# Gated-linear-attention and MoBA trunk on one core: the order of the first loads and of the first two projection blocks

## The chip, the cores and the metric

The kernel runs on one core of a Trainium2 chip. The metric is device time in microseconds (us) for one launch, the median of the runs of one program. The core has five instruction streams: TensorE (PE, matrix products into PSUM), VectorE (DVE), ScalarE (ACT), GpSimd (POOL) and SyncE (SP). They run apart and meet in semaphores. In this kernel SP and POOL do little else than issue DMA transfers, each on a queue of its own.

## What is computed

Two residual layers over x of 256 x 1024 in float32; layer 0 mixes with gated linear attention, layer 1 with MoBA attention, and each mixer is followed by a squared-ReLU MLP. Every sublayer is RMS-normed and modulated by vectors that come from c. The part that matters here is the beginning:

```python
c_act = jax.nn.silu(c)
mod = (c_act @ ada_w[i] + ada_b[i])[:, None, :]
sh1, sc1, g1, sh2, sc2, g2 = jnp.split(mod, 6, axis=-1)
h = rms_norm(x, norm_mix_g[i]) * (1 + sc1) + sh1
...
q, k, v, r, glr = jnp.split(h @ w_in, splits, axis=-1)
g = jax.nn.log_sigmoid((glr @ w_gate_up + b_gate).astype(f32)) / GLA_GATE_NORM
...
G = jnp.cumsum(g.reshape(B, NC, L, H, DK), axis=2)
q_dec = q * jnp.exp(G)
k_inv = k * jnp.exp(-G)
```

## The kernel before

**Tiling.** The 256 tokens are two tiles of 128 partitions, the contraction of 1024 is eight chunks of 128. A projection of 1024 by 512 columns is a *block* n; it is cut into four *units* u of two chunks each. Each weight number is split into a rounded part (`w_hi`, made on ACT, line 860) and the rest (`w_lo`, made on DVE, line 1186), the activations likewise (`a_hi`, `a_lo`), and three products are summed, so a unit costs 12 matmuls of 128 x 512 (lines 428 to 430, helper `three`). Units are counted through the whole kernel. `w_raw` holds four pieces of two units, `w_hi` and `w_lo` four units.

**Layer 0, mixer.** Blocks 0 to 5 are k, q, v, v, r, r (`MIX_IN`), 6 and 7 the output. Their results lie in PSUM banks 4 to 7, two for each block. Among the units, `sides` puts other TensorE work: for block 0, `second_mods` after unit 1 and `glr` after unit 3; for block 1, `logits` after unit 0 and `turn_k` after unit 2; then `turn_q`, `turn_tail`, `scores`, `update` and `output`. The gate's chain goes `glr` (TensorE), its copy (ACT, inside `k_in`), `logits` (TensorE), the bias and `z` (DVE `logits`), exp and ln (ACT `softplus`), the running sum (DVE `cumulate`), the exponentials (ACT `decays`), `keys` and `queries` (DVE), `scores` (TensorE). ACT and DVE have tables `tasks` that place these steps after a given (block, unit) of their splitting, and DVE a table `slots` with the places of the sums of the later modulation vectors (`ada`, lines 1201 and 1204), four instructions of 128 x 512 each.

**The modulation vectors of the first norm.** Four blocks of 512 columns of `ada_w` (0, 2, 1, 3 in this order, `ADA_PE`) are multiplied on TensorE: `ada_rows` gives rows spread over partitions 0, 32, 64 and 96 of one bank, ACT copies them (`ada_out`, line 900), and `ada_cols` sums them into columns. Blocks 0 and 2 belong to the first half of the channels (activation chunks 0 to 3, units 0 and 1 of every block), blocks 1 and 3 to the second half. `modulate` on ACT and DVE then makes `a_hi` and `a_lo`. Pieces of `w_raw` are called by block and half: piece (0, 0) holds units 0 and 1 of block 0.

**Queues.** SP issues, in this order: c, the identity, `ada_w` block 0, x, seven small vectors (`rows`), `ada_w` block 2, piece (0, 0), `ada_w` block 1, `ada_w` block 3, piece (0, 1), `constants` (the two gate weights `glr_w` and `glr_up`, masks, the restart vector of 512 KB, gate biases of 1 MB), then pieces (1, 0), (1, 1) and so on. POOL loads `ada_w` blocks from 4 on into `ada_raw`, as its halves come free.

## Time and profile before

| what | value |
| --- | --- |
| time, median of 3 runs | 687.27 us (686.78 to 690.5) |
| span of the profiled execution, first to last instruction | 686.4 us |
| lowest time minus that span | 0.4 us |
| TensorE busy | 646.6 us, 94% of the span |
| DVE busy | 470.6 us, 69% |
| ACT busy | 338.4 us, 49% |
| POOL busy | 30.3 us, 4% |
| DMA | 156.87 MB, mean 229 GB/s |
| mean granted TensorE clock | 0.980 |

No time of its own was taken of the profiled execution; its span stands for it, 0.4 us below the lowest time and 0.9 us below the median. Busy shares are averages over stages. The change touches the first tenth or so of the span; what it is worth there is read from the timelines of the three engines, from what each waited for, and from how long each transfer took to land. Times below are in us from the start of the span.

### The profile page before, as it was taken

How to read it: one execution, taken by the hardware profiler on the slowest of the kernel's cores; microseconds unless marked ns; L12 is line 12 of the kernel's file. 1: busy time of each engine (PE TensorE's matmuls, PEld its weight loads, DVE VectorE, ACT ScalarE, POOL GpSimd, SP SyncE). 2: the span in 40 equal slices, each digit the busy share in tenths (PEclk: the TensorE clock that was granted, in tenths of full speed). 3: DMA queues.
4: the chain of work that ended last, by engine and by line, in shares of the span. 5: the costliest groups of instructions: out<-in, count | busy, mean ns of one | idle time of the engine just before them, and what ended most of it. 6: DMA issues, size and time to landing. Idle time of an engine off the chain costs nothing.

```text
span 686.4 us, 9712 instructions
## 1 busy us (share of the span) xinstructions
PE 646.6 (94%) x3594; PEld 535.0 (78%) x3594; DVE 470.6 (69%) x702; ACT 338.4 (49%) x562; POOL 30.3 (4%) x44
## 2 busy tenths in 40 slices
PE   4789999999999999999997999989999999999997
PEld 2457866677789988998885666667779998999885
DVE  2358999696787877787886846685678844555446
ACT  3244632544854345435427756665585445443440
POOL 0011010000000000000000000000000000000000
PEclk9889999999999999999999999999999999999999
DMA  8999778554598877878935677760349555565501
GB/s 305 380 377 352 244 265 309 198 176 154 181 317 311 296 250 270 317 258 287 343 118 183 221 270 246 259 230 1 123 145 336 193 185 187 184 182 198 195 32 61
DMA packets 61492, 156.87 MB, mean 229 GB/s; under 512 B 4124, under 2 KB 5000, under 8 KB 61464
## 3 DMA queue, kind: packets, MB, share of 16 engines
q1 hardware_dynamic: 50584, 114.56, 48.3%
q0 software_dynamic: 10880, 41.95, 17.5%
q8 instruction: 17, 0.28, 0.2%
q14 instruction: 11, 0.09, 0.0%
HBM read 155.44 MB, written 1.05 MB: 228 GB/s over the span
## 4 chain that ended last, share of the span: by engine, by line
PE 77%; DVE 12%; ACT 6%; DMA 2%; issue 2%; SPq 1%; ACTq 0%; DVEq 0%; POOLq 0%
PE ps L428 16%; PE ps L429 15%; PE ps L430 15%; PE ps L582 8%; PE ps L581 8%; PE ps L580 8%; DVE w_lo L1186 3%; ACT w_hi L860 2%; PE ps L488 2%; DVE ada_acc L1204 1%; DMA rows<-in_ada_b_dram 1%; DMA ada_raw<-in_ada_w_dram 1%; DVE a_lo L1329 1%; PE ps L512 1%; PE ps L496 1%
## 5 line engine op out<-in xcount | busy, mean ns | idle before, releaser
L1186 DVE TENSOR_TENSOR w_lo<-w_raw,w_hi 128x1024 fp32r<-128x1024 f32 x192 | 232.4, 1222 | 140.7 <-ACT w_hi L860 140.5
L860 ACT ACTIVATE w_hi<-w_raw 128x1024 fp32r<-128x1024 f32 x192 | 200.4, 1057 | 222.7 <-PE ps L430 116.8
L428 PE MATMUL ps<-w_hi,a_hi 128*128 128x512 f32 x288 | 121.1, 421 | 20.1 <-DVE a_lo L1329 14.1
L580 PE MATMUL ps<-a_hi,w_hi 128*128 128x256 f32 x448 | 126.9, 283 | 0.0
L582 PE MATMUL ps<-a_hi,w_lo 128*128 128x256 f32 x448 | 126.8, 283 | 0.0
L581 PE MATMUL ps<-a_lo,w_hi 128*128 128x256 f32 x448 | 126.8, 283 | 0.0
L429 PE MATMUL ps<-w_lo,a_hi 128*128 128x512 f32 x288 | 116.0, 403 | 0.0
L430 PE MATMUL ps<-w_hi,a_lo 128*128 128x512 f32 x288 | 115.5, 401 | 0.0
L428 PE MATMUL ps<-w_hi,m_hi 128*128 128x512 f32 x256 | 100.7, 393 | 0.0
L429 PE MATMUL ps<-w_lo,m_hi 128*128 128x512 f32 x256 | 100.4, 392 | 0.0
L430 PE MATMUL ps<-w_hi,m_lo 128*128 128x512 f32 x256 | 100.3, 392 | 0.0
L428 PEld LDWEIGHTS ps<-w_hi,a_hi 128*128 128x128 f32 x288 | 56.2, 195 | 47.2 <-issue 16.9
L1204 DVE SCALAR_TENSOR_TENSOR ada_acc<-ada_raw,c_act,ada_acc 128x512 f32<-128x512 f32 (+1 forms) x112 | 84.0, 750 | 3.5
L581 PEld LDWEIGHTS ps<-a_lo,w_hi 128*128 128x128 f32 x448 | 85.9, 192 | 0.6
L580 PEld LDWEIGHTS ps<-a_hi,w_hi 128*128 128x128 f32 x448 | 85.9, 192 | 0.5
L582 PEld LDWEIGHTS ps<-a_hi,w_lo 128*128 128x128 f32 x448 | 85.9, 192 | 0.0
L430 PEld LDWEIGHTS ps<-w_hi,a_lo 128*128 128x128 f32 x288 | 56.2, 195 | 12.5
L429 PEld LDWEIGHTS ps<-w_lo,a_hi 128*128 128x128 f32 x288 | 56.3, 196 | 10.6 <-issue 0.2
L428 PEld LDWEIGHTS ps<-w_hi,m_hi 128*128 128x128 f32 x256 | 48.5, 190 | 11.2 <-issue 1.4
L430 PEld LDWEIGHTS ps<-w_hi,m_lo 128*128 128x128 f32 x256 | 48.5, 189 | 10.2
L429 PEld LDWEIGHTS ps<-w_lo,m_hi 128*128 128x128 f32 x256 | 48.5, 189 | 9.6
L284 POOL DMA_DIRECT2D ada_raw<-in_ada_w_dram x38 | 28.5, 749 | 452.5 <-DVE ada_acc L1204 359.0
(158 smaller groups left out, 509.1 us busy)
## 6 DMA issues: line engine op xcount, KB each, us to landing
w_raw<-in_mlp_w_dram SPq DMA_DIRECT2D x64, 1024.0 KB, 5.4
ada_raw<-in_ada_w_dram POOLq DMA_DIRECT2D x40, 1024.0 KB, 6.0
w_raw<-in_gla_w_in_dram SPq DMA_DIRECT2D x12, 1024.0 KB, 11.1
w_raw<-in_moba_w_in_dram SPq DMA_DIRECT2D x12, 1024.0 KB, 6.3
ada_raw<-in_ada_w_dram SPq DMA_DIRECT2D x4, 1024.0 KB, 10.8
arena<-in_ada_w_dram SPq DMA_DIRECT2D x4, 1024.0 KB, 12.8
w_raw<-in_gla_w_out_dram SPq DMA_DIRECT2D x4, 1024.0 KB, 7.7
w_raw<-in_moba_w_out_dram SPq DMA_DIRECT2D x4, 1024.0 KB, 5.1
```

The costliest lines, as they stand in the source:

```text
L284: nc.gpsimd.dma_start(ada_raw[:, half], src.rearrange("(k p) n -> p k n", p=P)).then_inc(ada_sw_in[half], 16)
L428: mm(out, hi, w_hi[:, slot, wc], start=first, stop=False)
L429: mm(out, hi, w_lo[:, slot, wc], start=False, stop=False)
L430: return mm(out, lo, w_hi[:, slot, wc], start=False, stop=last)
L488: z = mm(ps[32 * k:32 * k + 1, bank, :], c_act[:, 4 * half + k:4 * half + k + 1], raw[:, k], start=half == 0, stop=half == 1)
L496: z = mm(ps[:, bank, c0 + q:c0 + q + 1], ada_row[i // 4][:, i % 2, q * P:(q + 1) * P], ones[0:97, 0:1], start=True, stop=True)
L580: mm(o, w_hi[:, u, w], a_hi[:, a, :], start=u == 0 and k == 0, stop=False)
L581: mm(o, w_hi[:, u, w], a_lo[:, a, :], start=False, stop=False)
L582: z = mm(o, w_lo[:, u, w], a_hi[:, a, :], start=False, stop=u == 3 and k == 1)
L860: A(w_hi[:, c % SPLIT], w_raw[:, c // 2, c % 2], ACT.Copy).then_inc(hi_made, 1)
L1186: V.tensor_tensor(w_lo[:, c % SPLIT], w_raw[:, c // 2, c % 2], w_hi[:, c % SPLIT].bitcast(F32), ALU.subtract).then_inc(lo_made, 1)
L1204: z = V.scalar_tensor_tensor(acc, w, s, acc, op0=ALU.mult, op1=ALU.add)
```

## The change

- SP: x goes ahead of `ada_w` block 0. The order is now c, identity, x, `ada_w` 0, `ada_w` 2, piece (0, 0), `ada_w` 1, piece (1, 0), `ada_w` 3, piece (0, 1), piece (1, 1), and on from there.
- POOL: the seven small vectors are its first issues; the gate weights, then (behind `ada_w` block 4) the other constants and the gate biases follow.
- TensorE: x is transposed before the first `ada_rows`; the first two blocks run as (0,0), (0,1), (1,0), (1,1), (0,2), (0,3), (1,2), (1,3), with the `ada_rows` of block 1 after (0,1), those of block 3 and both `ada_cols` after (1,1), `glr` after (0,3), `logits` after (1,2).
- ACT: in `first_norm` it now does both x tiles first; the last two `ada_out` follow the splitting of units 2 and 3. The third and fourth row sums are in banks 0 and 1, and a column `sel` with ones in four partitions takes the place of `ones` in `ada_cols`.
- Tasks and slots of ACT and DVE in blocks 1 to 3 are moved to later units.

The order of ACT in the program, before. The stretch from the first `modulate` to the splits of units 4 and 5 (L860 is the split of a unit, L900 `ada_out`, L890 and L894 `modulate`):

```order
L894 ACTIVATE a_hi<-arena 128x512 [waits hD_ok,hA_ok]
L900 ACTIVATE arena<-ps 97x512 [waits col_T,ada_pe]
L860 ACTIVATE w_hi<-w_raw 128x1024 [waits raw_in1]
L860 ACTIVATE w_hi<-w_raw 128x1024
L900 ACTIVATE arena<-ps 97x512 [waits col_T,ada_pe]
L890 ACTIVATE arena<-ps,modc 128x256 [waits xT_ok,mod_ok]
L894 ACTIVATE a_hi<-arena 128x512 [waits hD_ok,hA_ok]
L890 ACTIVATE arena<-ps,modc 128x256 [waits xT_ok,mod_ok]
L894 ACTIVATE a_hi<-arena 128x512 [waits hD_ok,hA_ok]
L860 ACTIVATE w_hi<-w_raw 128x1024 [waits unit_used,raw_in2]
L860 ACTIVATE w_hi<-w_raw 128x1024 [waits unit_used]
```

The same stretch after the change (L883 is the split, L922 `ada_out`, L912 and L916 `modulate`):

```order
L916 ACTIVATE a_hi<-arena 128x512 [waits hD_ok,hA_ok]
L883 ACTIVATE w_hi<-w_raw 128x1024 [waits raw_in1]
L883 ACTIVATE w_hi<-w_raw 128x1024
L922 ACTIVATE arena<-ps 97x512 [waits col_T,ada_pe] x2
L912 ACTIVATE arena<-ps,modc 128x256 [waits xT_ok,mod_ok]
L916 ACTIVATE a_hi<-arena 128x512 [waits hD_ok,hA_ok]
L912 ACTIVATE arena<-ps,modc 128x256 [waits xT_ok,mod_ok]
L916 ACTIVATE a_hi<-arena 128x512 [waits hD_ok,hA_ok]
L883 ACTIVATE w_hi<-w_raw 128x1024 [waits unit_used,raw_in2]
L883 ACTIVATE w_hi<-w_raw 128x1024 [waits unit_used]
```

The row order hardly moved, but the units did: before, the two splits in front of the second `modulate` are units (0,2) and (0,3); now they are (1,0) and (1,1), and those of (0,2) and (0,3) stand behind it.

DVE before, from its `logits` (L1361, L1364) over `cumulate` (L1370 to L1375) and `keys` (L1383, L1384) to `queries` (L1390, L1393); L1186 is the split, L1201 and L1204 are `ada`:

```order
L1361 TENSOR_SCALAR arena<-ps,cols 128x256 x4
L1364 SCALAR_TENSOR_TENSOR arena<-arena 128x1024
L1201 TENSOR_SCALAR ada_acc<-ada_raw,c_act 128x512
L1204 SCALAR_TENSOR_TENSOR ada_acc<-ada_raw,c_act,ada_acc 128x512 x3
L1186 TENSOR_TENSOR w_lo<-w_raw,w_hi 128x1024
L1370 SCALAR_TENSOR_TENSOR arena<-arena 128x1024
L1372 SCALAR_TENSOR_TENSOR arena<-arena 128x1024
L1375 TENSOR_TENSOR arena<-arena 128x1024
L1186 TENSOR_TENSOR w_lo<-w_raw,w_hi 128x1024 x2
L1383 TENSOR_TENSOR arena<-ps,arena 128x512
```

DVE after, the same steps (L1382 and L1385 `logits`, L1391 to L1396 `cumulate`, L1404 `keys`, L1208 the split, L1223 and L1226 `ada`):

```order
L1382 TENSOR_SCALAR arena<-ps,cols 128x256 x4
L1385 SCALAR_TENSOR_TENSOR arena<-arena 128x1024
L1208 TENSOR_TENSOR w_lo<-w_raw,w_hi 128x1024
L1391 SCALAR_TENSOR_TENSOR arena<-arena 128x1024
L1393 SCALAR_TENSOR_TENSOR arena<-arena 128x1024
L1396 TENSOR_TENSOR arena<-arena 128x1024
L1208 TENSOR_TENSOR w_lo<-w_raw,w_hi 128x1024
L1404 TENSOR_TENSOR arena<-ps,arena 128x512
L1405 TENSOR_TENSOR arena<-ps,arena 128x512
L1404 TENSOR_TENSOR arena<-ps,arena 128x512
L1405 TENSOR_TENSOR arena<-ps,arena 128x512
L1208 TENSOR_TENSOR w_lo<-w_raw,w_hi 128x1024
```

The `ada` group left the place between `logits` and `cumulate`; it now stands behind `keys`, between the splits of units (3,0) and (3,1), and one split fewer stands between `cumulate` and `keys`.

TensorE after, from the program's start to the first product (L519 the transposes of x, L495 `ada_rows`, L503 `ada_cols`); before, the eight `ada_rows` of block 0 and the turn of `rows` came first and the sixteen transposes behind the first `ada_cols`:

```order
L519 MATMUL ps<-eye,arena 128x128 [waits xn_ok]
L519 MATMUL ps<-eye,arena 128x128 x7
L519 MATMUL ps<-eye,arena 128x128 [waits xn_ok]
L519 MATMUL ps<-eye,arena 128x128 x7
L495 MATMUL ps<-ada_raw,c_act 1x512 [waits ada_in0,set_up,c_ok]
...
L531 MATMUL ps<-eye,rows 128x100 [waits vec_in]
L495 MATMUL ps<-arena,c_act 1x512 [waits ada_pre_in0]
...
L503 MATMUL ps<-sel,arena 128x1 [waits row_ok]
...
L495 MATMUL ps<-arena,c_act 1x512 [waits ada_pre_in1]
...
L503 MATMUL ps<-sel,arena 128x1 [waits row_ok,vec_ok]
```

The transposes moved ahead of everything that waits for `ada_w`.

The diff, cut to what the text speaks of:

```diff
+    FIRST = [(0, 0), (0, 1), (1, 0), (1, 1), (0, 2), (0, 3), (1, 2), (1, 3)]
+    FIRST_DONE = [6, 8]
...
+            def vec(at, n, src):
+                nc.gpsimd.dma_start(rows[at:at + n, :], src).then_inc(vec_in, 16)
...
+            pool.wait_ge(ada_pe, 4)
+            with nc.allow_non_contiguous_dma(reason="sixteen columns"):
+                nc.gpsimd.dma_start(glr_w[:, :, :],
...
+            nc.gpsimd.dma_start(glr_up[:, :], gla_up[0]).then_inc(glr_in, 16)
             for half in range(2):
                 pool.wait_ge(ada_pe, 6 + half + 1)
                 nc.gpsimd.dma_start(ada_raw[:, half], ada_part(4, half)).then_inc(ada_sw_in[half], 16)
+            nc.gpsimd.dma_start(restart.rearrange("p a b -> p (a b)"), restart_d.to_broadcast([P, GH * SEQ])
+                                ).then_inc(con_in, 16)
...
+            for tb in range(TB):
+                sp.dma_start(x[:, tb], x_d[0, tb * P:(tb + 1) * P, :]).then_inc(x_in[tb], 16)
             for half in range(2):
                 load_ada(0, half)
-            for tb in range(TB):
-                sp.dma_start(x[:, tb], x_d[0, tb * P:(tb + 1) * P, :]).then_inc(x_in, 16)
...
+            load_pre(0, 2)
...
+                order = [(n, d) for n in range(MIX_BLOCKS) for d in range(2)]
+                if l == 0:
+                    order[1:3] = [(1, 0), (0, 1)]
...
+                    if l == 0 and i == 0:
+                        load_pre(1, 1)
+                    if l == 0 and i == 1:
+                        for half in range(2):
+                            load_ada(3, half)
...
             def first_norm():
+                for tb in range(TB):
+                    turn_norm(0, tb)
                 pe.wait_ge(c_ok, 1)
-                pe.wait_ge(set_up, 2)
+                pe.wait_ge(set_up, 3)
                 for half in range(2):
                     ada_rows(0, half, 6)
                 pe.wait_ge(vec_in, 16 * N_VEC)
                 tr(ps[:, 5, 0:N_ROWS], rows[0:N_ROWS, :], eye[0:N_ROWS, 0:N_ROWS]).then_inc(vec_T, 1)
+                ada_rows(2, 0, 7)
                 ada_cols(0, 4)
-                for tb in range(TB):
-                    turn_norm(0, tb)
-                for half in range(2):
-                    ada_rows(2, half, 7)
+                ada_rows(2, 1, 7)
...
+                def first_blocks(sides):
+
+                    for s, (n, u) in enumerate(FIRST):
+                        pe.wait_ge(lo_made, mix_base[0] + s + 1)
+                        if n == 0:
+                            pe.wait_ge(a_ok, u + 1)
...
+                first_blocks({1: lambda: second_rows(2), 3: lambda: (second_rows(3), second_cols()),
+                              5: glr, 6: logits})
...
-                    (1, 3): [k_in],
-                    (2, 0): [softplus],
+                    (2, 1): [k_in],
+                    (2, 2): [softplus],
...
-                    (2, 0): [logits], (2, 1): [cumulate], (2, 3): [keys], (3, 1): [queries, zero],
+                    (2, 1): [logits], (2, 2): [cumulate], (2, 3): [keys], (3, 1): [queries, zero],
...
-                slots = [(1, 0), (1, 2), (2, 0), (3, 1), (3, 2), (3, 3), (4, 0), (4, 2), (5, 0), (5, 2)]
+                slots = [(1, 3), (2, 0), (3, 0), (3, 1), (3, 2), (3, 3), (4, 0), (4, 2), (5, 0), (5, 2)]
```

## Rows read from the trace of the kernel before

**Rows 1.** The page's first part: busy us, share of the span, instructions of each engine.

```profile
PE 646.6 (94%) x3594; PEld 535.0 (78%) x3594; DVE 470.6 (69%) x702; ACT 338.4 (49%) x562; POOL 30.3 (4%) x44
```

**Rows 2.** Timeline of TensorE before the first product: start, duration, instruction, idle.

```profile
13.88 0.43 PE L522 MATMUL ps<-eye,rows 100*128 100x100 f32 x1 [2.21 <-DMA rows<-in_ada_b_dram]
...
15.71 3.65 PE L512 MATMUL ps<-eye,arena 128*128 128x128 f32 x16
19.30 2.90 PE L488 MATMUL ps<-arena,c_act 128*1 128x512 f32 x16
```

**Rows 3.** SP's issue of piece (0, 0), 8 to 9, and its time to landing.

```profile
L322 SPq DMA_DIRECT2D w_raw<-in_gla_w_in_dram x1: 1110/1110/1110, 8.1 to 8.1; - x1
...
DMA to landing us min/median/max: 13.1/13.1/13.1
```

**Rows 4.** Timeline of ACT, around both norms' halves and softplus.

```profile
22.76 1.99 ACT L860 ACTIVATE w_hi<-w_raw 128x1024 fp32r<-128x1024 f32 x2
...
43.44 0.63 ACT L894 ACTIVATE a_hi<-arena 128x512 fp32r<-128x512 f32 x1
...
63.56 1.06 ACT L962 ACTIVATE arena<-arena 128x1024 f32<-128x1024 f32 x1 [4.12 <-DVE arena L1364]
64.66 1.06 ACT L963 ACTIVATE arena<-arena 128x1024 f32<-128x1024 f32 x1
```

**Rows 5.** Timeline of TensorE, 27 to 66: where each stage of blocks 0 and 1 begins.

```profile
27.84 0.77 PE L428 MATMUL ps<-w_hi,a_hi 128*128 128x512 f32 x1 [3.80 <-DVE w_lo L1186]
...
35.21 1.90 PE L488 MATMUL ps<-arena,c_act 128*1 128x512 f32 x16
...
38.76 1.05 PE L496 MATMUL ps<-ones,arena 97*128 97x1 f32 x8
40.20 1.05 PE L496 MATMUL ps<-ones,arena 97*128 97x1 f32 x8 [0.39 <-ACT arena L900]
43.82 0.77 PE L428 MATMUL ps<-w_hi,a_hi 128*128 128x512 f32 x1 [2.57 <-DVE a_lo L1329]
...
51.72 3.63 PE L647 MATMUL ps<-arena,glr_w 128*16 128x256 f32 x16
...
60.14 0.50 PE L428 MATMUL ps<-w_hi,a_hi 128*128 128x512 f32 x1
...
65.73 1.04 PE L660 MATMUL ps<-eye,arena 128*128 128x128 f32 x8
```

**Rows 6.** Windows by time: PE, PEld, DVE, ACT, POOL busy, then granted clock, DMA.

```profile
46.00:48.00 2.00, 2.00 (x6) 1.54 (x6) 1.49 (x2) 1.43 (x2) 0.00 (x0) 0.50 1.03 385
104.00:105.00 1.00, 1.00 (x4) 0.71 (x4) 0.96 (x3) 0.00 (x0) 0.00 (x0) 0.50 1.01 401
```

**Rows 7.** Timeline of DVE, 60 to 80: `logits`, `ada`, `cumulate`, `keys`, `queries`.

```profile
60.62 1.65 DVE L1361 TENSOR_SCALAR arena<-ps,cols 128x256 f32<-128x256 f32 x4
62.30 1.23 DVE L1364 SCALAR_TENSOR_TENSOR arena<-arena 128x1024 f32<-128x1024 f32 x1
63.45 0.48 DVE L1201 TENSOR_SCALAR ada_acc<-ada_raw,c_act 128x512 f32<-128x512 f32 x1
63.96 2.33 DVE L1204 SCALAR_TENSOR_TENSOR ada_acc<-ada_raw,c_act,ada_acc 128x512 f32<-128x512 f32 x3
...
67.84 1.22 DVE L1370 SCALAR_TENSOR_TENSOR arena<-arena 128x1024 f32<-128x1024 f32 x1
...
72.56 2.35 DVE L1186 TENSOR_TENSOR w_lo<-w_raw,w_hi 128x1024 fp32r<-128x1024 f32 x2
74.83 0.68 DVE L1383 TENSOR_TENSOR arena<-ps,arena 128x512 f32<-128x512 f32 x1
...
79.58 1.28 DVE L1393 SCALAR_TENSOR_TENSOR arena<-ps,arena 128x512 f32<-128x512 f32 x2
```

**Rows 8.** Timeline of TensorE, 79 to 145: the first wait for DVE's state.

```profile
101.92 1.10 PE L700 MATMUL ps<-arena 64*128 64x256 f32 x6 [1.71 <-DVE arena L1416]
```

**Rows 9.** POOL's two loads of `ada_w` block 4, issued at 38.3 and 39.2.

```profile
DMA to landing us min/median/max: 9.0/10.6/12.2
```

More of the change, by code:

```diff
@@ L100, in trunk_kernel @@
         cols = sb("cols", [P, P])
+        sel = sb("sel", [P, 1])
         c_act = sb("c_act", [P, KC])
@@ L496, in ada_cols @@
                     z = mm(ps[:, bank, c0 + q:c0 + q + 1], ada_row[i // 4][:, i % 2, q * P:(q + 1) * P],
-                           ones[0:97, 0:1], start=True, stop=True)
+                           sel[0:97, :], start=True, stop=True)
                 z.then_inc(col_T, 1)
@@ L718, in output, with second_rows, second_cols @@
                     z.then_inc(o_p, 1)
-                def second_mods():
+                def second_rows(i):
+                    for half in range(2):
+                        ada_rows(ADA_FIRST[i], half, i - 2)
+                def second_cols():
                     for i in range(2, 4):
-                        for half in range(2):
-                            ada_rows(ADA_FIRST[i], half, 4 + i)
-                    for i in range(2, 4):
-                        ada_cols(i, 4 + i)
-                sides = [{1: second_mods, 3: glr},
-                         {0: logits, 2: turn_k},
-                         {1: turn_q, 2: turn_tail, 3: scores},
-                         {2: lambda: update(0), 3: lambda: update(1)},
+                        ada_cols(i, i - 2)
+                def first_blocks(sides):
[3 more added lines that the diff above has]
+                            pe.wait_ge(a_ok, u + 1)
+                        if (n, u) == (0, 2):
+                            pe.wait_ge(mod_red, 4)
+                        for k in range(2):
+                            for tb in range(TB):
+                                z = three(ps[:, in_bank(n, tb), :], a_hi[:, 2 * u + k, tile(tb)],
+                                          a_lo[:, 2 * u + k, tile(tb)], s % SPLIT, slice(k * COLS, (k + 1) * COLS),
+                                          u == 0 and k == 0, u == 3 and k == 1)
+                        z.then_inc(unit_used, 1)
+                        if s in sides:
+                            sides[s]()
+                sides = [None, None,
+                         {0: turn_k, 1: turn_q, 3: turn_tail},
+                         {0: scores, 2: lambda: update(0), 3: lambda: update(1)},
                          {0: lambda: update(2), 1: lambda: update(3), 2: lambda: output(0), 3: lambda: output(1)},
@@ L917, in first_norm @@
             def first_norm():
-                ada_out(0)
                 for tb in range(TB):
                     squares(0, tb)
-                ada_out(1)
+                for i in range(2):
+                    ada_out(i)
                 for u in range(2):
@@ L1657, in _ @@
             V.memset(ones[:, :], 1.0).then_inc(set_up, 1)
+            link(V.memset(sel[:, :], 0.0))
+            for k in range(4):
+                z = V.memset(sel[32 * k:32 * k + 1, :], 1.0)
+            z.then_inc(set_up, 1)
             V.memset(ps[:, 6:8, :], 0.0).then_inc(set_up, 1)
```

88 lines of the change are left out of this document (35 added, 53 removed).

## The prediction

> **What bounds the kernel now.** I read the page's busy shares first: TensorE works for 94% of the span, so 40 us are idle, and DVE is next with 69% [rows 1]. Such shares say nothing of a stage, so I went to TensorE's timeline of the first 66 us. Two gaps stand out there: 3.80 us before the first product at 27.84, and 2.57 us (with 0.39 just ahead) before the product of unit (0,2) at 43.82 [rows 5]. The third view is the timeline of DVE from 60 on: its rows join almost without a hole from `logits` to `queries` [rows 7], and TensorE's next long wait is one for DVE, 1.71 us before the `update` at 101.92 [rows 8]. So three things set the end of this stage in turn: transfers and the modulation up to 43.82, TensorE itself up to about 60, and then, although TensorE seems busy, the gate's chain on DVE up to 101.92. DVE has no slack there, and that decides this change. From 101.92 on nothing in the program is ordered otherwise, so whatever DVE is late or early there moves the end by as much.
>
> **The change, part 1: the start.** TensorE does the sixteen transposes of x (3.65 us) and waits 2.21 us for the small vectors ahead of the row sums of `ada_w` 2, which start at 19.30 and take 2.90 [rows 2]. Both leave the path. What is late next? Each half of those sums needs its own megabyte, landed by 19.30 at the latest, since no idle time stands there. In the new order only the second half (half of 2.90, 1.45 us) and ACT's copy of 0.6 stand behind that landing: 21.3. Piece (0, 0) was issued at 8.1 and took 13.1, so it is there at 21.2 [rows 3], and the bytes ahead of it are the same in both orders. ACT's first split begins at 22.76 now [rows 4] and at about 21.3 then. The gain is 22.76 - 21.3 = 1.5 us, and all that follows to the first product comes along: 27.84 becomes 26.3. I take 1.5. Its bounds are 0 (the vectors or x come no sooner than they are wanted) and 2.2 (the whole wait for the vectors, if the pieces land sooner as well).
>
> The small vectors go to POOL's queue. The nearest row is POOL's two loads of `ada_w` 4, issued while SP's queue was full: 9.0 and 12.2 us to landing [rows 9], for a megabyte each. If the last vectors, issued at about 6, took those 12.2, they would land at 18.2, TensorE would then turn them and do both halves of the sums (0.43 + 2.90, and the column sums of 1.05 between), and nearly all of the 1.5 us would be gone: 695.6 instead of the 694.3 below. I take no delay, because they are 8 KB and not 1024 KB each. By the Trainium skill (DMA: Bandwidth & Descriptors, section Queues, rings and completion order) each DMA engine takes turns between the queues it has work for, packet by packet, so small vectors on a queue of their own do not stand behind SP's megabytes; by that rule the gain stays whole. No row of before shows small transfers on POOL's queue.
>
> The memsets for `sel` are five more instructions on DVE in a stretch where it has nothing else to do. `sel` for `ones` changes no size. Both cost nothing; without that cover they would be well under 1 us.
>
> **Part 2: the first two blocks, interleaved.** From the first product to `glr` the program now takes 51.72 - 27.84 = 23.9 us [rows 5]. The new order, stage by stage, with the same rows: units (0,0), (0,1) 35.21 - 27.84 = 7.4; sums of `ada_w` 1, half of 38.76 - 35.21, 1.8; units (1,0), (1,1), 24 products at full clock, 65.73 - 60.14 = 5.6; sums of `ada_w` 3, 1.8; column sums, second `modulate`, up to the next product, 43.82 - 38.76 = 5.1; units (0,2), (0,3) 51.72 - 43.82 = 7.9. That is 29.6, so 5.7 us more ahead of `glr`. The 5.6 of them that are the moved units are no loss for TensorE, which does the work sooner, but they are a delay for all that waits for `glr`.
>
> Something is added. Before, units (0,2) and (0,3) are split ahead of the second `modulate`; now their splits are units 4 and 5 of ACT's and DVE's order and stand behind it. ACT's last `modulate` step ends at 44.07 [rows 4]; then the split on ACT takes 1.0 (half of 1.99) and its rest on DVE 1.2 (half of 2.35) [rows 4, 7]: 46.3 instead of 43.82, 2.5 us more. So TensorE's second gap does not close; it grows from 2.57 to about 5. The clock was at 0.50 after the present gap (46 to 48) [rows 6], which is the 1.2 GHz level, and the 7.9 above hold that cost already; it is paid again.
>
> `glr` therefore moves by 5.7 + 2.5 - 1.5 = 6.7 us. From it to the end of the `logits` products the pieces are the same as before (`glr`, one unit, `logits`, 8.4 us up to 60.14) [rows 5]. DVE picked the result up at 60.62, not 60.2, since it was busy with a split; then it will be waiting. So DVE's `logits` starts at 66.9, 6.3 later.
>
> **Part 3: the moved tasks.** Before, the `ada` group (63.45 to 66.29, 2.8 us) and a split lie between `logits` and `cumulate`, which starts at 67.84 although ACT's exp and ln were done at 65.72 [rows 4, 7]. In the new table only one split of 1.2 us lies there, so `cumulate` starts when ACT is done: 2.1 us less. Between `cumulate` and `keys` one split is left instead of two (2.35 us), but `keys` must wait for two of ACT's exponentials, of some 1.05 each like those of softplus [rows 4], so nothing is gained. Then the `ada` group comes ahead of `queries`: 2.8 us more. In sum +0.7. `queries`, over at 79.58 + 1.28 = 80.86 before [rows 7], is over at 80.86 + 6.3 + 0.7 = 87.9. TensorE now places `scores` after unit (3,0): by the stages above it is there at about 86, so it waits some 2 us for DVE. From `queries` on DVE's table is the old one, so the 7.0 us stay: `update` at 101.92 becomes 108.9, and the end moves by 7.0.
>
> The sum: -1.5 + 5.7 + 2.5 - 0.4 + 0.7 = +7.0 us on the profiled span of 686.4, which was 0.4 below the lowest time and 0.9 below the median. On the median: 687.27 + 7.0 = 694.3.
>
> **Part 4: POOL's other transfers.** The masks, the restart vector and the gate biases, 1.9 MB, leave the space ahead of pieces (1, 0) and (1, 1), and stand behind `ada_w` 4 on POOL. First user is `cumulate`, at about 72; they are issued near 44. At 395 GB/s [rows 6] they take 4.8 us, so they are hidden. The first `ada` of DVE wants `ada_w` 4 at about 52: issued at about 42, it lands between 51 and 54 [rows 9]. DVE then has about 4 us free before `logits` at 66.9, which covers that.
>
> **The rivals.** (1) Only TensorE's own work counts, and DVE catches up. One split less stands behind `logits`, and DVE idles before it, which speaks for it; the closed rows of DVE and the wait at 101.92 speak against it. Then the end moves by -1.5 + 0.1 + 2.5 = +1.1: 688.4. (2) Faster. TensorE arrives at the `update` with 5.6 us of work done in advance, so if DVE's chain were not late, the wait of 1.71 [rows 8] and the slow clock behind it (0.50 at 104 [rows 6], nine products at 0.43 instead of 0.23 us, 1.8) would vanish: 688.4 - 3.5 = 684.9, and 684.2 with the larger start gain. It decides from the point at which `glr` moves by less than DVE's gain of 2.1; I find 6.7, so this needs the two units before `glr` to be nearly free. (3) It does not do what it says: the first product comes at 27.8 as before, because vectors or x hold it. Then 687.27 + 8.5 = 695.8. (4) POOL's queue becomes the bound: `ada_w` 4 lands late, because the gate weights (64-byte runs) and SP's pieces share the engines with it, DVE stands in its order, and the splits queued behind that `ada` keep TensorE waiting. With one more landing time of the shorter kind left over after the 4 us of cover, 9.0 - 4 - 2 = 3 us: 697.3.
>
> **Chances.** Forecast 0.66, with 692.3 to 696.3 as its own range; rival (1) 0.12; (2) 0.07; (3) 0.07; (4) 0.08. About 0.5%, 3.4 us, is what a measurement of this kernel can tell from no change. Slower by more than that is above 690.7: forecast, (3) and (4), 0.81. Within it are (1) and most of (2), 0.15. Faster by more is 0.04. The range goes from 690.0, which takes in the upper part of (1), to 698.0, which takes in (3) and (4).
>
> **What would show it.** In the new profile: the first product near 26.3; a second gap of about 5 us before unit (0,2) at about 50.5, put down to a split (`w_lo`) and no longer to `a_lo`; `glr` near 58.4; DVE's `logits` near 66.9 with some 4 us idle ahead; TensorE waiting about 2 us for `queries` at `scores`; the first `update` that waits for the state near 108.9; and equal stages from there. The forecast is wrong if the interleaved units run while the clock stays at full speed without a second gap, if `logits` comes before 64, or if DVE reaches `queries` with slack.

## The result

The changed kernel takes 694.06 us, the median of 4 runs (692.91 to 695.7); the kernel before took 687.67 in the 4 runs beside it (686.78 to 690.5). The ratio is 1.0081, 95% interval 1.0051 to 1.011: slower by 0.8%. Between the medians that is 6.4 us, by the ratio 5.6 us (3.5 to 7.6). The forecast was 694.3. In the profiled executions the span grew by less, from 686.4 to 691.7, 5.3 us; where the rest went is one of the questions below. The profiled execution of after took 693.48 us, so 1.8 us of it lie outside the span.

The first row of its page, to be held against [rows 1]. TensorE is busy for less time than before in a span that is longer, so the loss is idle time and not work:

```profile
PE 644.0 (93%) x3594; PEld 532.8 (77%) x3594; DVE 471.1 (68%) x707; ACT 338.6 (49%) x562; POOL 38.4 (6%) x59
```

The timeline of TensorE after: start, duration, instruction, and in brackets the idle time before it with what ended it. Line numbers are those of after (L435 is the first product of a unit, L654 `glr`, L691 `scores`, L707 `update`, L718 `output`):

```profile
14.34 0.31 PE L531 MATMUL ps<-eye,rows 100*128 100x100 f32 x1
...
26.46 0.77 PE L435 MATMUL ps<-w_hi,a_hi 128*128 128x512 f32 x1 [4.90 <-DVE w_lo L1208]
...
43.09 1.95 PE L503 MATMUL ps<-sel,arena 97*128 97x1 f32 x16
50.11 0.79 PE L435 MATMUL ps<-w_hi,a_hi 128*128 128x512 f32 x1 [5.07 <-DVE w_lo L1208]
...
57.51 3.63 PE L654 MATMUL ps<-arena,glr_w 128*16 128x256 f32 x16
...
86.99 2.05 PE L691 MATMUL ps<-arena 128*128 128x128 f32 x16 [1.71 <-DVE arena L1414]
...
98.65 2.07 PE L707 MATMUL ps<-arena 64*128 64x256 f32 x6 [3.41 <-DVE arena L1426]
...
118.05 0.70 PE L718 MATMUL ps<-arena 128*128 128x256 f32 x2 [0.36 <-DVE arena L1437]
```

Against [rows 5] and [rows 8]: the first product comes 1.4 us earlier; the second gap has doubled and is put down to a split, `w_lo`; `glr` is 5.8 us later; TensorE waits for `queries` at `scores`. One row is not in the prediction at all: the wait of 3.41 us at the first `update`, for `masked` (L1426).

DVE's timeline after (L1382 `logits`, L1391 `cumulate`, L1223 the first of an `ada` group, L1414 `queries`, L1426 `masked`, L1437 the state), to be held against [rows 7]:

```profile
66.04 1.66 DVE L1382 TENSOR_SCALAR arena<-ps,cols 128x256 f32<-128x256 f32 x4 [4.51 <-PE ps L660]
71.17 1.23 DVE L1391 SCALAR_TENSOR_TENSOR arena<-arena 128x1024 f32<-128x1024 f32 x1 [1.08 <-ACT arena L985]
...
81.67 0.48 DVE L1223 TENSOR_SCALAR ada_acc<-ada_raw,c_act 128x512 f32<-128x512 f32 x1
...
85.65 1.28 DVE L1414 SCALAR_TENSOR_TENSOR arena<-ps,arena 128x512 f32<-128x512 f32 x2
...
93.37 0.49 DVE L1223 TENSOR_SCALAR ada_acc<-ada_raw,c_act 128x512 f32<-128x512 f32 x1 [1.20 <-DMA ada_raw<-in_ada_w_dram]
97.27 1.32 DVE L1426 COPY_PREDICATED arena<-keep,ps 128x512 f32<-128x512 int32 x2
...
103.47 0.49 DVE L1223 TENSOR_SCALAR ada_acc<-ada_raw,c_act 128x512 f32<-128x512 f32 x1 [0.75 <-DMA ada_raw<-in_ada_w_dram]
108.35 0.48 DVE L1437 SCALAR_TENSOR_TENSOR arena<-arena,dec,ps 128x256 f32<-128x256 f32 x1
```

DVE is idle for 4.5 us ahead of `logits`, since TensorE brings its input late. From there to the state its holes are short, the longest of them 1.20 us. The state is ready at 108.8; before, at 101.8.

Two windows of 2 us each at the end of the next norm, in after and then in before (PE, PEld, DVE, ACT, POOL busy, then granted clock, DMA share, GB/s):

```profile
160.00:162.00 2.00, 2.00 (x16) 1.85 (x16) 1.97 (x5) 0.00 (x0) 0.00 (x0) 1.00 0.97 369
162.00:164.00 2.00, 2.00 (x11) 1.62 (x10) 1.93 (x4) 0.00 (x0) 0.00 (x0) 1.00 0.94 342
```

```profile
154.00:156.00 2.00, 2.00 (x9) 1.71 (x9) 1.93 (x5) 0.00 (x0) 0.00 (x0) 0.62 1.00 395
156.00:158.00 2.00, 2.00 (x6) 1.51 (x6) 1.79 (x3) 0.00 (x0) 0.00 (x0) 0.53 1.03 388
```

It is the same work in both. Before, the clock was at its lower level for most of 4 us, which costs (1 - 0.62) x 2 + (1 - 0.53) x 2 = 1.7 us; in this execution of after it stayed at full speed. From 134.7 up to that place TensorE's rows are 6.7 us late, behind it 5.1 us. So the forecast of +7.0 was nearly met up to here, and 1.6 us came back through the clock in this one execution.

### The profile page after: what moved, and what is told of

It reads as the page before. It is cut to its first block, busy times and chain, and to the rows that moved or that the text cites. A ratio compares the mean times of both kernels' runs of the same rounds, so it can differ in the third digit from the quotient of the medians.

```text
span 691.7 us, 9715 instructions
## 1 busy us (share of the span) xinstructions
PE 644.0 (93%) x3594; PEld 532.8 (77%) x3594; DVE 471.1 (68%) x707; ACT 338.6 (49%) x562; POOL 38.4 (6%) x59
## 4 chain that ended last, share of the span: by engine, by line
PE 75%; DVE 12%; ACT 5%; DMA 4%; issue 2%; SPq 1%; ACTq 0%; POOLq 0%; DVEq 0%
PE ps L435 16%; PE ps L436 15%; PE ps L437 15%; PE ps L589 8%; PE ps L588 8%; PE ps L587 8%; DVE w_lo L1208 3%; DMA w_raw<-in_gla_w_in_dram 2%; DMA ada_raw<-in_ada_w_dram 2%; PE ps L495 2%; ACT w_hi L883 1%; DVE ada_acc L1226 1%; DVE a_lo L1350 1%; PE ps L718 1%; DVE x L1362 1%
## 5 line engine op out<-in xcount | busy, mean ns | idle before, releaser
L1208 DVE TENSOR_TENSOR w_lo<-w_raw,w_hi 128x1024 fp32r<-128x1024 f32 x192 | 232.4, 1223 | 130.5 <-ACT w_hi L883 130.3
L883 ACT ACTIVATE w_hi<-w_raw 128x1024 fp32r<-128x1024 f32 x192 | 200.3, 1057 | 227.8 <-PE ps L437 122.1
L435 PE MATMUL ps<-w_hi,a_hi 128*128 128x512 f32 x288 | 121.0, 420 | 24.1 <-DVE w_lo L1208 12.6
L435 PE MATMUL ps<-w_hi,m_hi 128*128 128x512 f32 x256 | 100.7, 393 | 0.0
L435 PEld LDWEIGHTS ps<-w_hi,a_hi 128*128 128x128 f32 x288 | 55.8, 194 | 52.5 <-issue 17.2
L1226 DVE SCALAR_TENSOR_TENSOR ada_acc<-ada_raw,c_act,ada_acc 128x512 f32<-128x512 f32 (+1 forms) x112 | 84.0, 750 | 3.5
L435 PEld LDWEIGHTS ps<-w_hi,m_hi 128*128 128x128 f32 x256 | 48.5, 190 | 11.2 <-issue 1.4
```

The lines of the kernel that those rows point to most:

```text
L435: mm(out, hi, w_hi[:, slot, wc], start=first, stop=False)
L883: A(w_hi[:, c % SPLIT], w_raw[:, c // 2, c % 2], ACT.Copy).then_inc(hi_made, 1)
L1208: V.tensor_tensor(w_lo[:, c % SPLIT], w_raw[:, c // 2, c % 2], w_hi[:, c % SPLIT].bitcast(F32), ALU.subtract).then_inc(lo_made, 1)
L1226: z = V.scalar_tensor_tensor(acc, w, s, acc, op0=ALU.mult, op1=ALU.add)
```

## The experiments

Each experiment was timed in 5 rounds beside the kernel before on the same chip; ratios are to that one, and 0.1% is 0.7 us. The row of after is the measurement above. The theory is that of the prediction: DVE's chain from `logits` to the state, which now begins late, sets the end. Its main rival is that only TensorE's own gap counts.

| kernel | ratio to before (95% interval) | span |
| --- | --- | --- |
| after | 1.0081 (1.0051 to 1.0110) | 691.7 |
| e1_start_only | 1.0017 (0.9997 to 1.0036) | 686.6 |
| e2_interleave_only | 1.0106 (1.0086 to 1.0126) | 693.0 |
| e3_split_ahead | 1.0049 (1.0032 to 1.0067) | 689.6 |
| e4_ada_in_gap | 1.0063 (1.0042 to 1.0083) | 692.8 |
| e6_before_ada_late | 0.9943 (0.9924 to 0.9963) | 683.3 |
| e7_start_ada_late | 0.9976 (0.9962 to 0.9990) | 685.6 |
| e8_after_ada_late | 0.9989 (0.9973 to 1.0005) | 689.8 |
| e10_glr_first | 0.9922 (0.9901 to 0.9942) | 682.1 |
| e11_start_table_late | 0.9933 (0.9911 to 0.9955) | 684.5 |
| e12_start_const_late | 0.9933 (0.9907 to 0.9959) | 683.8 |
| e13_split_ada_late | 0.9956 (0.9934 to 0.9979) | 683.2 |
| e14_const_on_pool | 0.9971 (0.9952 to 0.9991) | 687.4 |

**The two halves of the change.** e1 is the kernel before with the new start alone (x first, small vectors on POOL, x turned first; the constants stay on SP's queue):

```diff
+            for tb in range(TB):
+                sp.dma_start(x[:, tb], x_d[0, tb * P:(tb + 1) * P, :]).then_inc(x_in[tb], 16)
             for half in range(2):
                 load_ada(0, half)
...
+                for tb in range(TB):
+                    turn_norm(0, tb)
                 pe.wait_ge(c_ok, 1)
```

> The kernel before with the start of the change alone (x first, small vectors on POOL, transposes first), blocks 0 and 1 not interleaved, constants still on SP. Theory (DVE's chain, fed by the pieces of block 1, ends the stage): the first product comes at 26.4 instead of 27.84, but pieces (1, 0) and (1, 1) land at 45 and 52 as before, DVE closes up behind them, the update that waits for the state is at 101.5 to 101.9, and the end moves by 0 to -0.5 us. Rival (the start gain is passed on whole, as it was in the changed kernel): the update is at 100.4 and the end moves by -1.4 us.

Its first product comes at 26.59, 1.25 us earlier than before, and its state is waited for until 102.02, later than before [rows 8]:

```profile
102.02 1.10 PE L700 MATMUL ps<-arena 64*128 64x256 f32 x6 [1.86 <-DVE arena L1414]
```

The gain is made and does not arrive. At `glr` it is already gone (51.67 against 51.72), and in this trace all of it went on TensorE, without a wait: units (0,0) and (0,1) took 8.2 us instead of 7.4, units (0,2) and (0,3) 8.3 instead of 7.9. The clock stayed at its lower level for longer. The window from 30 to 32, in e1 and then in before:

```profile
30.00:32.00 2.00, 2.00 (x6) 1.52 (x6) 0.00 (x0) 0.00 (x0) 0.00 (x0) 0.50 1.05 386
```

```profile
30.00:32.00 2.00, 2.00 (x7) 1.53 (x7) 0.00 (x0) 0.00 (x0) 0.00 (x0) 0.60 1.05 386
```

The time of e1 is 1.2 us above before, with an interval from -0.2 to +2.5. That leaves out the rival's -1.4 and takes in the upper end of the theory's range (0), but the trace does not show the theory's reason: DVE's `logits` starts 8.9 us behind `glr` as in before, so DVE was not late by itself. The trace is of one of the three shortest of the twelve executions of e1 (688.3 us; the median is 690.78), so what makes the others longer it does not show.

e2 is the changed kernel with the old start:

> The changed kernel with the old start (ada_w 0 ahead of x, small vectors on SP, transposes behind the first sums); interleaving, tasks, slots and constants as changed. Theory: first product at 27.8, glr 1.4 us later than in the changed kernel (58.9), and the end 1.4 us above the changed kernel, +7.8 us over the kernel before. Rival (the start has no part in it): the end is that of the changed kernel, +6.4.

It is 0.25% above after, with intervals that overlap, so the times alone don't tell the theory from its rival. In the trace each mark from the first product on (27.61) is 1.2 us later than in after: `glr` 58.66, DVE's `logits` 67.18, and the span is 1.3 us longer. The row of its second gap:

```profile
51.28 0.80 PE L436 MATMUL ps<-w_hi,a_hi 128*128 128x512 f32 x1 [5.08 <-DVE w_lo L1209]
```

So the loss is the interleaving's (1.06% alone, 7.3 us), and in the traces the start gains its 1.2 us there, where it does not gain in e1.

**The size of the second gap.** e3 puts the splits of units (0,2) and (0,3) back ahead of the second `modulate`:

```diff
-                for i in range(2, 4):
-                    ada_out(i)
+                ada_out(2)
+                for u in range(4, 6):
+                    hi_at(u)
+                ada_out(3)
...
-                for u in range(2, 4):
+                for u in range(2, 6):
```

> The changed kernel with the splits of units (0,2) and (0,3) moved ahead of the second modulate on ACT and DVE. Theory: the gap before unit (0,2) shrinks from 5.1 to 2.6 us, glr starts at 55.0 instead of 57.5, DVE's logits, queries and the update all come 2.5 us sooner, and the end 2.5 us below the changed kernel (691.6). Rival (TensorE's own work is the bound and the chain on DVE is not): the gap shrinks, but waits further on grow by the same amount and the end stays within 0.7 us.

```profile
47.56 0.47 PE L435 MATMUL ps<-w_hi,a_hi 128*128 128x512 f32 x1 [2.53 <-DVE a_lo L1353]
```

The gap is 2.53 again and put down to `a_lo` again, and the kernel gains 0.32%, 2.2 us. The unit comes 2.55 us earlier than in after, and all of that is the gap: the first product is 0.9 us earlier (25.53), but TensorE is slower behind it, and the column sums begin at 43.09 in both. The difference has some 2.4 us either way; e13 against e8 below makes the same edit and gives 2.3 us with 1.9 either way. The two together confirm the term of 2.5 us as a cause.

**The chain on DVE.** e4 moves the `ada` group that now stands ahead of `queries` into DVE's idle time before `logits`:

```diff
-                    (2, 1): [logits], ...
+                    (2, 1): [lambda: ada(5, 0), logits], ...
```

> The changed kernel with one ada group (ada_w 5, first half) moved from behind keys to ahead of DVE's logits, where DVE sits idle for 4.5 us. Theory (DVE's chain decides): logits is at most 0.8 us later, queries about 2.0 us sooner (85.0 instead of 86.9), and the end about 2 us below the changed kernel (692.1). Rival (TensorE is the bound, scores has slack): queries comes sooner, the end stays within 0.5 us. Rival (the load of ada_w 5 is late, since it stands behind the constants on POOL's queue): logits waits for it, 2 us or more later, and the end rises.

```profile
65.57 0.49 DVE L1223 TENSOR_SCALAR ada_acc<-ada_raw,c_act 128x512 f32<-128x512 f32 x1 [4.64 <-DMA ada_raw<-in_ada_w_dram]
```

The idle time is there, but the data is not: this `ada_w` block lands at 65.5, so `logits` starts at 68.34 instead of 66.04 and most of the 2.8 us is given back. The verdict on the time is open, since its interval overlaps that of after. What it shows is that the hole on DVE is no free place, as the queue that fills it is as late as the hole.

e6, e8 and e13 take the opposite way: the groups go behind the chain. Only the table changes, in e6 of the kernel before, in e8 of after, and in e13 of e3:

```diff
-                slots = [(1, 0), (1, 2), (2, 0), (3, 1), (3, 2), (3, 3), (4, 0), (4, 2), (5, 0), (5, 2)]
+                slots = [(1, 0), (1, 2), (2, 0), (3, 1), (3, 3), (4, 0), (4, 2), (5, 0), (5, 1), (5, 2)]
...
-                slots = [(1, 3), (2, 0), (3, 0), (3, 1), (3, 2), (3, 3), (4, 0), (4, 2), (5, 0), (5, 2)]
+                slots = [(1, 3), (2, 0), (3, 1), (3, 3), (4, 0), (4, 2), (5, 0), (5, 1), (5, 2), (5, 3)]
```

> The kernel before with one ada group taken off DVE's closed stretch: the places (3, 2) and (3, 3) become (3, 3) and (4, 0), and so on, the last new one being (5, 1), so that four groups and not five lie between logits and the state; nothing else. Theory (DVE's chain ends the stage at 101.92): the state comes about 3 us sooner, the 1.7 us wait at the update and the slow clock behind it go, and the end moves by -2.5 to -4 us. Rival (TensorE is the bound of the stage, DVE's wait is incidental): the wait goes but the end moves by less than 1 us.

> The changed kernel with the ada groups moved off DVE's stretch (places (1, 3), (2, 0), (3, 1), (3, 3), (4, 0), (4, 2), (5, 0), (5, 1), (5, 2), (5, 3)); interleaving and start as changed. Theory (of the 6.4 us most is the chain on DVE, and 2.5 is the late split on TensorE): queries comes 2.9 us sooner, the waits at scores and at the first update go or shrink, and the end falls by 5 to 6.5 us, to 0 to +1.5 over the kernel before. Rival (TensorE's own longer way is the main part): the end falls by less than 3 us.

> The changed kernel with both the splits of units (0,2) and (0,3) ahead of the second modulate (as in e3_split_ahead) and the later ada table of e8_after_ada_late. Theory: the 2.2 us of the splits and the 6.4 us of the table add up, since each is on the path and neither hides the other: ratio to before 0.995 to 0.996. Rival: with DVE given slack by the table TensorE is the bound, and the split's 2.5 us come only in part or, by TensorE's own gap, still in full; if they come in no part the ratio stays at 0.9989.

In e6 the third `update` starts with no wait:

```profile
100.21 1.13 PE L700 MATMUL ps<-arena 64*128 64x256 f32 x6
```

It saves 0.57%, 3.9 us, where the chain's wait and the slow products behind it came to 1.7 + 1.7 us in the trace of before. In e8 `glr` and `logits` are even 1.4 us later than in after (58.87 and 67.39), and yet DVE ends `masked` at 92.9 instead of 98.6, and the wait of 3.41 us is gone:

```profile
84.24 1.28 DVE L1414 SCALAR_TENSOR_TENSOR arena<-ps,arena 128x512 f32<-128x512 f32 x2
...
91.55 1.35 DVE L1426 COPY_PREDICATED arena<-keep,ps 128x512 f32<-128x512 int32 x2
```

```profile
93.83 1.13 PE L707 MATMUL ps<-arena 64*128 64x256 f32 x6
...
102.52 1.10 PE L707 MATMUL ps<-arena 64*128 64x256 f32 x6 [0.62 <-DVE arena L1437]
```

e8 is 0.92% below after, 6.3 us, which is as much as the whole change cost. That is the strongest single proof of the theory: the same late `glr`, the same work on TensorE, and the time falls when DVE has less in its chain. The rival, by which TensorE's gap alone counts, would have left e8 at after's time. It does not say that the interleaving is free once DVE has slack, since the same edit also helps before, by 3.9 us. With the late table in both, e8 is 0.46% or 3.2 us above e6, where after is 0.81% above before. e13 adds the splits on top: 0.9956, 0.33% or 2.3 us below e8, where e3 saved 2.2 us. Within the noise, some 2 us for each such difference, the two add up.

**Why the start's gain was lost.** e7 was meant to be e1 with the late table, and its expectation speaks of that. The kernel that ran was another: it had the table of before, and on top of e1 the constants on POOL's queue as in after. Its expectation therefore can't be judged by it.

> The start of the change (as in e1) on the kernel before, with DVE relieved as in e6 (places (3, 1), (3, 3), (4, 1), (4, 3), (5, 0), (5, 1), (5, 2)). Theory (what ate the start gain in e1 was DVE's chain): with DVE out of the way the start gain of some 1.3 us shows, the end lies 3.5 to 5 us below the kernel before. Rival (the landing of pieces (1, 0) and (1, 1), or the clock of TensorE at the start, ate it): the end is that of e6 within 0.5 us.

What ran is an answer to another question, though: it differs from e1 in the queue of the constants alone, and is 0.41% (2.8 us) shorter. e14 makes that edit alone on the kernel before, and e11 and e12 are the two kernels with the late table, with the constants on SP and on POOL:

> The kernel before with one edit: gate weights, masks, restart vector and gate biases go on POOL's queue as in the changed kernel, everything else (x, small vectors, order of blocks, tables) as before. e7 against e1 differs by this alone and was 2.8 us shorter. Theory (pieces (1,0) and (1,1) land sooner because 1.9 MB are out of SP's queue ahead of them, so splits of block 1 stop waiting): 1 to 3 us below before, ratio 0.996 to 0.9985. Rival (that difference was the granted clock after the second gap, which was at 0.93 in e7 and at 0.50 in e1 at 46 to 48, and has nothing to do with the constants): same as before, 0.9990 to 1.001.

> The kernel before with x as the first big load, the small vectors on POOL's queue and x turned first (as in e1_start_only, constants on SP), and with the table of the ada groups as in e6_before_ada_late: (1,0) (1,2) (2,0) (3,1) (3,3) (4,0) (4,2) (5,0) (5,1) (5,2). It is the kernel that the expectation of e7_start_ada_late speaks of; the table was left as before there. Theory (the start's 1.5 us were eaten in e1 by DVE's closed chain and by the wait for the state): with slack on DVE the start gain reaches the end, 1 to 2 us below e6_before_ada_late, ratio to before 0.9915 to 0.993. Rival (it is eaten by the slower granted clock after the first products, 0.50 for longer, whatever DVE does): same as e6_before_ada_late, 0.994 or above.

> The kernel e7_start_ada_late as it ran (new start, constants on POOL's queue, ada table as before) with the late ada table of e6_before_ada_late. Theory: the two gains add, the late table gives again some 4 us on 687.6, ratio to before 0.9920, and the wait of 1.57 us for the state that e7's trace shows at 99.8 is gone. Rival: e7 was already limited by TensorE and the transfers, so the late table gives less than 1.5 us there: 0.995 or above.

The constants stand on SP's queue ahead of pieces (1, 0) and (1, 1). ACT's split of piece (1, 0), in e1, e11 and e14 in turn; in before the wait was 1.36 us and ended at 45.43:

```profile
47.44 2.01 ACT L860 ACTIVATE w_hi<-w_raw 128x1024 fp32r<-128x1024 f32 x2 [3.83 <-DMA w_raw<-in_gla_w_in_dram]
```

```profile
50.29 2.00 ACT L860 ACTIVATE w_hi<-w_raw 128x1024 fp32r<-128x1024 f32 x2 [8.25 <-DMA w_raw<-in_gla_w_in_dram]
```

```profile
43.81 1.99 ACT L860 ACTIVATE w_hi<-w_raw 128x1024 fp32r<-128x1024 f32 x2
```

SP issues piece (1, 0) at 35.24 in before and at 34.5 in e1 and e11, behind the constants, of which `glr_w` and `glr_up` (64 and 32 KB) alone hold its queue for 2.6 and 5.5 us. In e14 the pieces (0, 1), (1, 0) and (1, 1) follow each other from 20.73 on. With the new start and the constants on SP the piece lands later than before, not sooner. DVE stands behind it with its splits and two `ada` groups, and in e11 that eats the slack it had: its `logits` starts at 62.85, 2.2 us later than before, although `glr` came 1.9 us earlier.

```profile
51.38 1.22 DVE L1185 TENSOR_TENSOR w_lo<-w_raw,w_hi 128x1024 fp32r<-128x1024 f32 x1 [8.61 <-ACT w_hi L860]
...
62.85 1.65 DVE L1359 TENSOR_SCALAR arena<-ps,cols 128x256 f32<-128x256 f32 x4
```

In e12 there is no such wait and `logits` starts at 58.68, 1.9 us earlier than before, and queries keep that gain. The third `update` and the turned tiles of the next norm (136.54 in e12, 138.54 in e6) are 2.0 us earlier than in e6. In e7, with the table of before, DVE is the bound again, and TensorE waits 1.57 us for the state until 99.81; but that is 2.1 us earlier than in before, so there the gain has come as far as the state.

So the traces show two ways in which the start's gain goes: TensorE's lower clock behind the first products (e1), and the late piece when the constants are on SP (e11). The wait for the state alone does not take it (e7). The times bear that out only in part. The queue of the constants is worth 2.8 us with the old table (e1 to e7) and nothing with the late one (e11 and e12 have the same ratio), as it should be if the late piece acts through a DVE without slack. But e11 and e12 are only 0.1% below e6, where 1 to 2 us were expected of the start: 0.7 us, with 2.2 us either way by the two intervals. And e7 against e14, which differ in the start alone, gives 0.3 us the other way, with 1.7 us either way. In the trace of e12 the 2.0 us shrink to 0.4 by 163.3, since the slow clock of the stretch between cost 3.4 us there and 1.7 in e6.

The clock is the rival named ahead of e11, and the mean granted clocks of all executions speak for it. In the old order the new start goes with the lower one each time: 0.9751 for 0.9798 (e1 and before beside it), 0.9778 for 0.9808 (e7 and e14), 0.9798 and 0.9790 for 0.9811 (e11 and e12 against e6). On TensorE's 646 us that is worth 3.0, 1.9, 0.8 and 1.4 us (an estimate), beside the 1.6 us by which the first product came earlier. The last two pairs come from different sessions. Why the clock is lower there no run shows. What the start is worth at the end of the kernel in the old order stays open.

e14 is 2.1 us shorter than before, with an interval from 0.6 to 3.3. Its profiled execution does not show where: `update` still waits 1.69 us, up to 102.21. What differs is the spread. The 31 runs of before beside it went from 686.97 to 692.56, the 12 of e14 from 686.7 to 689.04. I take it that piece (1, 0) lands later in some executions of before than in the profiled one, as it does in e1 and e11, and then delays DVE. The rival is the granted clock, and it is not settled. Its mean over the 12 runs of e14 is 0.0016 higher than over those 31, worth 1.1 of the 2.1 us on TensorE's 646 us (an estimate). But it accounts for less than half of the spread: the longer half of the 31 is 3.4 us above the shorter half and its clock is 0.0024 lower, worth 1.5 us, and in e1 the longer half is 3.1 us above the shorter at the same 0.975. So part of what makes an execution long is waiting. That it is waiting for this piece is argued from the spread and from three landings, not shown, since there is no trace of a slower execution of before.

**A better order.** e10 takes the theory to its end: the gate's chain must start as early as it can. It has the interleaved blocks, but `glr` stands right behind the second `modulate` and ahead of unit (0,2), `logits` behind (0,2), their partners on DVE one place and on ACT two to four places earlier, and the late table with its first group at (1, 0). The diff, cut to TensorE's order:

```diff
-                first_blocks({1: lambda: second_rows(2), 3: lambda: (second_rows(3), second_cols()),
-                              5: glr, 6: logits})
+                first_blocks({1: lambda: second_rows(2), 3: lambda: (second_rows(3), second_cols(), glr()),
+                              4: logits})
```

> The changed kernel with glr put into the gap before unit (0,2) (it needs the modulated activations, not the splits) and logits after unit (0,2), their partners on ACT and DVE two to five units sooner, and ada groups off DVE's stretch as in e8. Theory (the interleaving hurts by what it puts ahead of glr): glr begins at about 47.5 instead of 57.5, the gap of 5 us is filled, DVE's logits comes at about 60, no wait for DVE is left on TensorE before 115, and the end is 4 to 6 us below the kernel before. Rival (DVE has too much work ahead of the state wherever glr stands): waits of 2 us and more stay, and the end is not below that of the kernel before.

```profile
47.90 2.66 PE L657 MATMUL ps<-arena,glr_w 128*16 128x256 f32 x6 [2.41 <-ACT arena L915]
```

```profile
58.48 1.65 DVE L1385 TENSOR_SCALAR arena<-ps,cols 128x256 f32<-128x256 f32 x4
```

```profile
101.98 1.13 PE L710 MATMUL ps<-arena 64*128 64x256 f32 x6
```

`glr` starts 9.6 us earlier than in after and stands where the second gap was, of which 2.41 us are left, and none of the four `update` steps waits. At 0.9922, 684.1 us (683.62 to 684.48), it is faster than both kernels, by 0.8% or 5.4 us than before and by 1.6% than after. It is the lowest ratio of all, though e11 and e12 are within its interval.

## Why the prediction was right

The time is 694.06 against 694.3. That they are so close is in part luck: the 7.0 us forecast for the difference stand against 6.4 us between two medians of 4 runs, 5.6 us by the ratio and 5.3 us in the profiled pair, and two terms were off by 1.0 us each and cancelled. What the traces confirm is the chain, step by step, each against the trace of after:

| step | forecast | measured |
| --- | --- | --- |
| first product | 26.3 | 26.46 |
| first product to the column sums | 16.6 | 43.09 - 26.46 = 16.6 |
| column sums to unit (0,2) | 5.1 + 2.5 = 7.6 | 50.11 - 43.09 = 7.0 |
| (0,2) and (0,3) | 7.9 | 57.51 - 50.11 = 7.4 |
| `glr` to DVE's `logits` | 8.9 - 0.4 = 8.5 | 66.04 - 57.51 = 8.5 |
| `logits` to `cumulate` | 2.1 less | 5.13 for 7.22, 2.1 less |
| `cumulate` to the end of `queries` | 2.8 more | 15.76 for 13.02, 2.7 more |
| end of `queries` to the state | as before | 21.9 for 20.9, 1.0 more |
| state ready | +7.0 | 108.83 for 101.77, +7.1 |

**The start** was right in size. ACT's first split began at 21.38, where 21.3 was forecast, and what it waited for was piece (0, 0):

```profile
21.38 2.00 ACT L883 ACTIVATE w_hi<-w_raw 128x1024 fp32r<-128x1024 f32 x2 [0.99 <-DMA w_raw<-in_gla_w_in_dram]
```

The single pair of traces would not carry the 1.5 us: over the fourteen traces the first product comes at 25.5 to 26.6 with the new start and at 26.7 to 27.8 with the old one (before, e2, e6, e14), 1.6 us apart on the mean. POOL's queue was no risk: the seven small vectors, issued there between 1.4 and 5, land in at most 5.9 us, so that TensorE turns them at 14.34 without waiting. For the line that issues them (L285):

```profile
DMA to landing us min/median/max: 2.5/4.9/5.9
```

The bound of 12.2 us from the megabyte loads [rows 9] was far off. That fits the reason given, their size, but no run separates it from the time of issue: the vectors were issued by 5, and SP's issues took long only from then on (3.5 us for piece (0, 0), 5.7 for the two behind it). By the rule of the Trainium skill named in the prediction (DMA: Bandwidth & Descriptors, Queues, rings and completion order) a queue of their own would keep the small loads from standing behind the megabytes. The traces agree: on SP's queue, in before, the last vector was issued at 6.6 and TensorE waited for it until 13.88 [rows 2], 7.3 us, where none took more than 5.9 on POOL's. That the gain also reaches the end holds in the traces of the interleaved order (e2 against after) and not in those of the old one (e1 against before).

**The interleaving** was right in mechanism and about 1 us too high in size. The column sums now run as one group, without the 0.39 us that stood between them before [rows 5], which the 5.1 contained. And the slow phase behind the gap was shorter, 7.4 us for the two units. The second is no property of the order: other executions show 7.2 to 8.4 for these units.

**The moved tasks** were right to 0.1 us each, and that they stand on the path is what e6 and e8 show.

**A miss that cancelled.** I wrote that from `queries` on DVE's table is the old one, so that the 7.0 stay. The table was the same, but the loads behind it were not on time: two `ada` groups waited 1.20 and 0.75 us for `ada_w`, in before one waited 0.96. That is 1.0 us more on DVE and makes up for the 1.0 above. A group that comes earlier in the table asks for its data earlier; I had gone through that only for the first one.

**A wait that I did not see.** The expected wait for the state near 108.9 did not come, since TensorE had already waited 3.41 us for `masked` at 98.65. `masked` stands on DVE behind two groups and two splits after `queries`, so it moved by the same 7 us as all of DVE, and TensorE, which reaches the first `update` at 95.2, meets it first. For the sum it is the same: whichever step of the chain is met first, TensorE falls in behind DVE. It also takes more of the low clock:

```profile
99.00:105.00 6.00, 6.00 (x16) 4.29 (x15) 5.07 (x8) 0.00 (x0) 0.75 (x1) 0.50 1.00 371
```

That is 3.0 us behind this wait, where it was 1.7 us behind the shorter one of before.

**The end.** I let all 7 us stand to the end. In the profiled pair 5.1 arrived, as the slow phase of before at 154 to 158 was missing in after. In the medians 6.4 arrived. I also set the span of before beside its lowest time as if 0.4 us lay outside it. In the profiled executions of after and of all experiments it is 1.6 to 2.0, and in all 78 later executions of before 1.6 or 1.7, so the profiled one of before took about 688.1 us (an estimate). As the forecast was a difference, nothing hung on it.

**The rivals.** That only TensorE counts (1) falls by e8. Its time would be seen if DVE had slack: e8 against e12, which differ in the interleaving and both have the late table, gives +3.9 us (with some 2 us either way), of which e13 puts 2.3 on the splits and leaves 1.6 for the rest; rival (1) had +2.6 for the interleaving. Faster (2) needed a chain that was not late; e6 and e10 are what it looks like. The missing start (3) was refuted by the first product. Rival (4) had `ada_w` block 4 late on POOL's queue. That block came in time; loads behind it were late, which cost 1.0 us and not 3, and in e4, which asks for block 5 earliest, 4.64.

**Part 4, the constants,** was right in that their first users don't wait (its 395 GB/s stand between the 385 and 401 of [rows 6] and in neither). It left out a gain: it priced what the 1.9 MB do on POOL's queue, not what their leaving SP's does for the pieces behind them. The edit alone, in e14, is worth 2.1 us (0.6 to 3.3), though its way to the end is not shown.

## What to carry to other kernels

An idle hole or a busy share says where an engine stands, not what it is waiting for; here the engine with 94% was led by the one with 69%. When an order is changed to fill a gap of the busiest engine, look first at which result of the moved stretch feeds the longest chain on another engine, and keep that result's work in front: with the late table in both, the interleaved kernel with `glr` in front of unit (0,2) and its partners moved up with it (e10) is 0.67% (4.6 us) faster than the one with `glr` behind (0,3) (e8). Work without a due time (here the `ada` groups) belongs behind such a chain; that edit of one table was worth 4 to 6 us, nearly as much as the interleaving cost (7.3) and more than the start ever gained.

## What the runs showed of the hardware

The granted clock makes executions of the same work differ. Windows of the trace of e12, at the place where before lost 1.7 us and after nothing, show the lower level (0.50 is 1.2 GHz) for longer:

```profile
150.00:152.00 2.00, 2.00 (x6) 1.52 (x6) 1.93 (x5) 0.00 (x0) 0.00 (x0) 0.50 1.01 393
152.00:154.00 2.00, 2.00 (x6) 1.59 (x5) 0.84 (x2) 0.00 (x0) 0.00 (x0) 0.50 1.06 389
154.00:156.00 2.00, 2.00 (x7) 1.55 (x6) 0.00 (x0) 0.00 (x0) 0.00 (x0) 0.68 1.01 373
```

With the third row these are 2.6 us, and with the windows of 1 us around them 3.4. So this place alone costs 0, 1.7 or 3.4 us in different traces. Summed over the whole span in windows of 1 us, (1 - clock) times TensorE's busy time is 7.8 to 14.0 us in the fourteen traces (an estimate; a part of it lies beside other waits). A difference of 2 us between two single traces therefore says little until the clock of both has been laid side by side; it is one reason why e14's gain can be seen in 12 runs and not in its trace. The other is that its trace is of the longest of the twelve (689.04), and that of before of one of its shorter ones (about 688.1).

The same wait is not always followed by the same clock. Before the third `update`, TensorE waits 1.71 us in before, 1.86 in e1, 1.57 in e7 and 1.69 in e14. In the first three the clock falls to 0.50 behind it; in e14 it does not:

```profile
103.00:107.00 4.00, 4.00 (x20) 2.85 (x18) 3.82 (x8) 0.71 (x1) 0.00 (x0) 1.00 1.01 398
```

What an issue on SP costs does not go by the size of its transfer: in before that of `glr_up`, 32 KB, took 5.5 us behind `glr_w` and the megabytes, and those of the four transfers after it, 64 to 512 KB, 0.4 us each.
